# Dilated attention: the q/k tiles of two of the three dilations turned by DMA transposes and kept in token order

## The chip, the cores and the metric

The kernel runs on one core of a Trainium2 chip. The metric is device time in microseconds (us) of one execution, the median of the runs. The engines are TensorE (PE in the rows, its weight loads PEld), VectorE (DVE), ScalarE (ACT), GpSimd (POOL) and SyncE (SP), which issues most DMAs.

## The reference

A trunk of two layers over 256 tokens of width 1024, in fp32: a sparse attention layer, then a dilated attention layer, each followed by a gated feed-forward block. The change touches the dilated layer alone. It projects the normed input to q, k and v of 16 heads of 64 for each of three dilations (1, 4, 16), turns the first 16 elements of each q and k head by position, and lets each token see the tokens of its own residue class within a window. The three outputs are joined with the softmax of their log sums, which is one softmax over all three sets of scores.

```python
DIL_PATTERNS = ((128, 1), (512, 4), (2048, 16))
proj = (a @ w_in).reshape(B, S, N_DIL, 3, H, DH)
for gi, (window, dil) in enumerate(DIL_PATTERNS):
    q = partial_rope(proj[:, :, gi, 0], cos, sin)
    k = partial_rope(proj[:, :, gi, 1], cos, sin)
    v = proj[:, :, gi, 2]
    o, lse = banded_attention(to_residue(q, dil)[:, :, :, None], to_residue(k, dil),
                              to_residue(v, dil), window // dil)
    ...
alpha = jax.nn.softmax(jnp.stack(lses, axis=-1), axis=-1)
o = jnp.einsum('bshn,bshnd->bshd', alpha.astype(a.dtype), jnp.stack(outs, axis=3))
return o.reshape(B, S, H * DH) @ w_o
```

## The kernel before

Every large product is made as three matmuls of fp32r parts: each weight piece (1 MB, a slot of a ring of seven in w_raw) is split by ScalarE into a high part (w_hi, L735) and by VectorE into a low part (w_lo, L1256), two halves each. SyncE issues the loads of the pieces in order; each waits until the piece seven before it has been used. ScalarE splits a piece three ahead of the tile that TensorE works on.

The dilated layer takes its 16 heads in four groups of four. A group has tiles of 128 tokens by 512 columns, each of 24 matmuls (gemm, L1830): six q/k tiles, two for each dilation (pat 0, 1 and 2 stand for dilations 1, 4 and 16), two tiles of v for pat 0 and 1, and in groups 0 and 2 two more v tiles for pat 2. There are 36 tiles in all, numbered e. The first group takes its q/k tiles in the order pat 1, 2, 0, the others 1, 0, 2, so that in those the tiles of pat 2 come last. For v tiles the stationary operand, the turned input, is read with a step of two elements (8 bytes).

A q/k tile goes this way. ScalarE evacuates it from PSUM to stage_dil (L1103, two slots), VectorE applies the rotation in place (L1688 to L1695), TensorE turns it with four transposes in the middle of the next tile's matmuls (dil_turn, L1839), and ScalarE evacuates the turned tile (dil_turn_out, L1127 to L1136) into qk_t, in an order in which the tokens of a class lie together, with q scaled. For pat 0 the high parts go to qk_hi, and VectorE makes the low parts from PSUM and qk_hi (dil_turn_lo, L1708 and L1713).

Scores are made for 16 units, four to a group (dil_scores): a unit is two heads by 128 queries. It has eight matmuls of 64x64 in fp32 for the residue classes of pat 1 and 2 (class matmuls), whose k is read with a step of two elements, and six of 64x128x256 in fp32r for pat 0. Scores of a group are made among the tiles of the next group; those of the last group among the output projection's matmuls, the first after 18 of these with the last tile's turn in their middle. VectorE masks the scores and finds the least (L1451), ScalarE takes the exponential, VectorE divides, TensorE turns the probabilities and multiplies them with v.

GpSimd has no work in the dilated layer but two DMAs. It stores the residual h to h_rows, waits, and loads it back in another order of rows (h_permuted), which VectorE needs when it adds the output projection. In the two feed-forward blocks a hidden tile of 128x256 is turned without TensorE: GpSimd splits it into two planes of 16 bits (split_hidden, L683), ScalarE issues a DMA transpose (L1018), GpSimd merges the planes (merge_hidden, L691).

## Time and profile before

| | us |
|---|---|
| median of 3 runs | 810.12 (810.08 to 810.49) |
| profiled execution, its device time | 810.76 |
| its span, first to last instruction | 809.0 |
| dilated layer in it, tiles and attention | about 342 to 616 |

The profile is of one execution of its own. Its span leaves out some 1.8 us ahead of and behind the instructions. A duration in a timeline row runs from start to modelled end, and neighbours on TensorE overlap, so the time that one costs is read from the starts around it.

### The profile page before, as it was taken

What the parts mean: (1) busy time and instruction counts of PE and PEld (TensorE: products, weight loads), DVE (VectorE), ACT (ScalarE), POOL (GpSimd) and SP (SyncE); (2) the same over time, 40 slices, a digit from 0 to 9 for tenths busy, and PEclk for the clock granted to TensorE, in tenths of its full rate; (3) what the DMA queues carried; (4) which work ended last, traced back from release to release, by engine and by line L of the source; (5) the groups of instructions that cost most, each with busy time, mean ns of one, the idle gap of its engine ahead of it and who ended that gap; (6) DMA issues with size and microseconds to landing.
All of it is one profiled execution on the core that took longest, in us unless ns stands there. A gap on an engine that the chain in (4) does not pass through costs nothing.

```text
span 809.0 us, 11869 instructions
## 1 busy us (share of the span) xinstructions
PE 798.6 (99%) x4401; PEld 643.8 (80%) x4401; DVE 528.5 (65%) x1121; ACT 457.5 (57%) x879; POOL 102.2 (13%) x167
## 2 busy tenths in 40 slices
PE   9999999999999999999999999999999999999996
PEld 7877675788888888788888888888877888888885
DVE  6966969796565556697566665766668775655644
ACT  7836877765444444575555566555658554444431
POOL 1000005812212221000000000000000112222210
PEclk9999999999999999999999999999999999999998
DMA  9955211168886687658544535363424688678811
GB/s 318 351 184 200 86 54 53 59 189 241 242 212 191 191 238 216 188 198 269 157 157 153 160 121 192 105 208 105 157 88 172 191 248 224 173 197 236 236 21 52
DMA packets 128490, 142.24 MB, mean 176 GB/s; under 512 B 25856, under 2 KB 111920, under 8 KB 128304
## 3 DMA queue, kind: packets, MB, share of 16 engines
q1 hardware_dynamic: 107760, 132.53, 52.6%
q10 hardware_dynamic: 19680, 4.75, 3.6%
q0 software_dynamic: 992, 4.19, 1.4%
q8 instruction: 35, 0.57, 0.3%
q14 instruction: 23, 0.19, 0.1%
HBM read 134.64 MB, written 2.10 MB: 169 GB/s over the span
## 4 chain that ended last, share of the span: by engine, by line
PE 96%; DVE 2%; ACT 1%; issue 0%; POOL 0%; ACTq 0%; POOLq 0%
PE ps L1830 86%; PE ps L1839 6%; PE ps L2107 2%; PE ps L2080 2%; PE ps L2118 1%; PE ps L1892 1%; ACT junk L756 0%; DVE w_lo L1256 0%; ACT xd_hi L744 0%; ACT w_hi L735 0%; ACT probs_b L907 0%; DVE h L1580 0%; DVE h L1586 0%; DVE tmp L1584 0%; ACT p_t L922 0%
## 5 line engine op out<-in xcount | busy, mean ns | idle before, releaser
L1256 DVE TENSOR_TENSOR w_lo<-w_raw,w_hi 128x1024 fp32r<-128x1024 f32 x240 | 295.5, 1259 | 64.8 <-ACT w_hi L735 62.5
L735 ACT ACTIVATE w_hi<-w_raw 128x1024 fp32r<-128x1024 f32 x240 | 245.5, 1060 | 3.0 <-DMA w_raw<-in_ffn_w_gu 2.9
L1830 PE MATMUL ps<-w_hi,xt_hi 128*128 128x512 f32 x472 | 188.5, 401 | 0.3 <-ACT w_hi L735 0.3
L1830 PE MATMUL ps<-w_hi,xt_lo 128*128 128x512 f32 x472 | 183.5, 390 | 0.0
L1830 PE MATMUL ps<-w_lo,xt_hi 128*128 128x512 f32 x472 | 183.0, 390 | 0.0
L1830 PE MATMUL ps<-w_hi,xd_hi 128*128 128x512 f32 x288 | 117.4, 408 | 0.2 <-DVE w_lo L1256 0.2
L1830 PE MATMUL ps<-w_hi,xd_lo 128*128 128x512 f32 x288 | 113.2, 393 | 0.0
L1830 PE MATMUL ps<-w_lo,xd_hi 128*128 128x512 f32 x288 | 112.8, 392 | 0.0
L1830 PEld LDWEIGHTS ps<-w_hi,xt_hi 128*128 128x128 f32 x472 | 88.5, 188 | 25.0 <-issue 8.6
L1830 PEld LDWEIGHTS ps<-w_hi,xt_lo 128*128 128x128 f32 x472 | 88.6, 188 | 18.9
L1830 PEld LDWEIGHTS ps<-w_lo,xt_hi 128*128 128x128 f32 x472 | 88.7, 188 | 16.7 <-DVE w_lo L1256 0.3
L1002 ACT ACTIVATE silu<-ps,rs 128x256 f32<-128x256 f32 x44 | 20.9, 475 | 91.6 <-PE ps L1830 87.9
L1830 PEld LDWEIGHTS ps<-w_hi,xd_lo 128*128 128x128 f32 x288 | 54.7, 190 | 11.8
L1830 PEld LDWEIGHTS ps<-w_hi,xd_hi 128*128 128x128 f32 x288 | 54.8, 190 | 11.2 <-DVE w_lo L1256 0.4
L1830 PEld LDWEIGHTS ps<-w_lo,xd_hi 128*128 128x128 f32 x288 | 54.9, 191 | 9.8
L1830 PE MATMUL ps<-w_hi,st_hi 128*128 128x512 f32 x160 | 62.6, 391 | 0.0
L1830 PE MATMUL ps<-w_hi,st_lo 128*128 128x512 f32 x160 | 62.3, 389 | 0.0
L1830 PE MATMUL ps<-w_lo,st_hi 128*128 128x512 f32 x160 | 62.3, 389 | 0.0
L691 POOL COPY ht<-planes_t 128x512 uint16<-128x512 uint16 x36 | 33.4, 928 | 212.1 <-DMA planes_t<-planes 212.1
L1594 DVE SCALAR_TENSOR_TENSOR hs<-ps,rs,silu 128x256 f32<-128x256 f32 x44 | 21.3, 483 | 51.9 <-ACT silu L1002 51.9
L1012 ACT ACTIVATE st_hi<-ht 128x256 fp32r<-128x256 f32 x36 | 15.0, 416 | 70.8 <-PE ps L1830 42.1
L1600 DVE TENSOR_TENSOR st_lo<-ht,st_hi 128x256 fp32r<-128x256 f32 x36 | 15.2, 422 | 48.2 <-ACT st_hi L1012 48.2
(271 smaller groups left out, 984.9 us busy)
## 6 DMA issues: line engine op xcount, KB each, us to landing
w_raw<-in_ffn_w_gu SPq DMA_DIRECT2D x88, 512.0 KB, 5.6
w_raw<-in_dil_w_in SPq DMA_DIRECT2D x72, 512.0 KB, 4.6
w_raw<-in_ffn_w_down SPq DMA_DIRECT2D x44, 512.0 KB, 5.4
w_raw<-in_nsa_w_in SPq DMA_DIRECT2D x20, 512.0 KB, 7.3
w_raw<-in_nsa_w_o SPq DMA_DIRECT2D x8, 512.0 KB, 4.8
w_raw<-in_dil_w_o SPq DMA_DIRECT2D x8, 512.0 KB, 4.5
w_k<-in_nsa_cmp_wk SPq DMA_DIRECT2D x2, 1024.0 KB, 9.0
w_raw<-in_nsa_cmp_wv SPq DMA_DIRECT2D x2, 1024.0 KB, 11.5
```

The lines of the kernel that those rows point to most:

```text
L691: pool.tensor_copy(halves_of(ht[:, j % 2, m, :]), view(planes_t, (j % 2 * MT + m) * 512, [[256, 2], [1, 256]])).then_inc(ht_merged, 1)
L735: act.activation(w_hi[:, n.slot, c:c + 1024], w_raw[:, n.slot, c:c + 1024], ACT.Copy)\
L1002: act.activation(silu[:, m, :], bank(gu_bank(j, m), 0, 256), ACT.Silu, scale=rs[:, m:m + 1])\
L1012: act.activation(view(st_of(j)[0], m * P, [[S, 2], [1, P]]), ht_from(j, m), ACT.Copy)\
L1256: dve.tensor_tensor(w_lo[:, n.slot, c:c + 1024], w_raw[:, n.slot, c:c + 1024], w_hi[:, n.slot, c:c + 1024].bitcast(F32), ALU.subtract)\
L1594: dve.scalar_tensor_tensor(hs[:, m, :], bank(gu_bank(j, m), 256, 256), rs[:, m:m + 1], silu[:, m, :], ALU.mult, ALU.mult).then_inc(hs_read ...
L1600: dve.tensor_tensor(view(st_of(j)[1], m * P, [[S, 2], [1, P]]), ht_from(j, m), hi.bitcast(F32), ALU.subtract).then_inc(ht_ready, 1)
L1830: ins = pe.matmul(o, s, m, start=start, stop=stop, **kw)
L1839: ins = pe.transpose(ps[0:n, b, P * k:P * k + P], src, ident[:, 0:P])
L1892: pe.transpose(bank(3, 0, P), ident[:, 0:P], ident[:, 0:P])
L2080: pe.matmul(bank(score_bank(odd), 0, 2 * n), q_t[rows, hd // 2, m * P:(m + 1) * P], k_both[rows, :, hd // G, 0:n], start=True, stop=True). ...
L2107: pe.matmul(view(ps, OT_BANK * 512 + P * j, [[1, P]], p0=DH * odd, n=DH), v_nsa[:, i // (m + 1), i % (m + 1), hk * DH:(hk + 1) * DH], p_t2 ...
```

## The change

The 16 q/k tiles of pat 0 and 1 (BARS) are no longer turned by TensorE; the eight of pat 2 (PE_TURNS) still are. After the rotation GpSimd splits a tile of 128x512 fp32 into two planes (split_qk, 128x1024 of 16 bits), SyncE issues a DMA transpose of both planes at a fixed place among the weight loads (turn_planes, called by load), and GpSimd merges the result into qk_t, in token order (merge_qk). The planes are laid over h, so h is stored to h_rows in two parts (save_h) and loaded back when the last merge is done.

The scores read the classes of pat 1 by steps of four elements, for q and for k. For pat 0, ScalarE and VectorE make the high and low parts of a whole group's q and k once the last merge of the group is done (first_q_hi, first_lo_out, first_k_hi): q into an order in which its columns stay contiguous for the scores, k in token order, read with a step of two elements. The scale of q moves from the evacuation to the mask operation, and the constants of the mask change with it. The first scores of a group wait for the merges and for the evacuation of the pat 2 tiles, and those of pat 0 for the low parts.

```diff
@@ -117,27 +117,29 @@
 
 
 XBAR = [(1, 0), (1, 1)] + [(j, m) for j in range(2, FJ - 1) for m in range(MT)]
+DIL_BARS = 2 * MT * DIL_G
...
 def xbar_no(layer, j, m):
 
-    return len(XBAR) * layer + XBAR.index((j, m))
+    return (len(XBAR) + DIL_BARS) * layer + XBAR.index((j, m))
...
 
     tiles = [x for x in XBAR if x[1] == m]
-    return len(tiles) * layer + tiles.index((j, m)) + 1
+    return (len(tiles) + DIL_BARS // 2) * layer + tiles.index((j, m)) + 1
...
-N_TURNS = sum(x.kind == QK for x in TILES)
-
-
-def firsts_until(qk_no):
-
-    return sum(x.kind == QK and x.pat == 0 and x.qk_no <= qk_no for x in TILES)
+BARS = [x for x in TILES if x.kind == QK and x.pat < 2]
+PE_TURNS = [x for x in TILES if x.kind == QK and x.pat == 2]
+
+
+def bar_at(x):
+
+    return len(XBAR) + BARS.index(x)
...
-        h = sb("h", [P, MT, D])
+        at_h = zone(MT * D * 4)
+        h = sb("h", [P, MT, D], at=at_h)
+        planes_q = sb("planes_q", [P, 2, 1024], U16, at=at_h)
+        planes_qt = sb("planes_qt", [P, 2, 8, P], U16, at=at_h + 4096)
...
-        qk_hi = sb("qk_hi", [P, 4, 4, S], F32R, at=at_a)
+        k_parts = sb("k_parts", [P, 4, 2, 2, S], F32R, at=at_a)
...
-        qk_lo = [sb(f"qk_lo{i}", [P, S], F32R, at=at) for i, at in
-                 enumerate((at_gp + 3072, at_s + 9216, at_tmp + 3072, at_tmp + 7168))]
+        q_hi, q_lo = ([sb(f"q_{k}{hp}", [P, S], F32R, at=at) for hp, at in enumerate(homes)] for k, homes in
+                      (("hi", (at_gp + 3072, at_s + 9216)), ("lo", (at_tmp + 3072, at_tmp + 7168))))
...
+        def first_q_whole(g, hp):
+
+            return view(qk_t, (qk_slot(g, 0) * 4 + hp) * S, [[1, 2], [2, 2], [4, 64]])
+
+        def first_q_part(t, hp):
+
+            return view(t[hp], 0, [[P, 2], [64, 2], [1, 64]])
...
+            def turn_ahead_of(x):
+
+                return N_DIL + ({0: 7, 2: 10}[x.e] if x.e < 4 else 2 * x.chunk + 8 + x.m)
+
+            def turn_planes(n):
+
+                for i, x in enumerate(BARS):
+                    if turn_ahead_of(x) != n:
+                        continue
+                    if i == 0:
+
+                        sp.wait_ge(h_saved, 16 * MT)
+                        sp.wait_ge(xt_psum[2], 2 * MT)
+                        sp.wait_ge(sq_h[2], MT)
+                    sp.wait_ge(planes_ready, bar_at(x) + 1)
+                    sp.dma_start_transpose(planes_qt[:, i % 2, :, :], planes_q[:, i % 2, :])\
+                      .then_inc(planes_turned[i % 2], 16)
+
             def load(pc, *parts):
 
+                turn_planes(pc.n0)
...
+            def split_qk(x):
+
+                pool.wait_ge(roped[1], x.qk_no + 1)
+                pool.tensor_copy(view(planes_q, BARS.index(x) % 2 * 1024, [[512, 2], [1, 512]]),
+                                 halves_of(stage_dil[:, x.qk_no % 2, :])).then_inc(planes_ready, 1)
+
+            def merge_qk(x):
+
+                i, pos = BARS.index(x), qk_order(x.g).index(x.pat)
+                pool.wait_ge(planes_turned[i % 2], 16 * (xbar_of(0, FJ - 2, i % 2) + i // 2 + 1))
+
+                if x.g - (pos == 0) > 0:
+                    pool.wait_ge(scores[1], 8 * (x.g - (pos == 0)))
+                to = qk_t[:, qk_slot(x.g, x.pat), :, x.m * P:(x.m + 1) * P].bitcast(U16)
+                pool.tensor_copy(to.rearrange("p b (i k) -> p k b i", k=2),
+                                 view(planes_qt, i % 2 * 1024, [[512, 2], [P, 4], [1, P]])).then_inc(ht_merged, 1)
+
+            def save_h(m):
+
+                for half in range(2):
+                    pool.wait_ge(h_ready[2][half], m + 1)
+                pool.dma_start(h_rows[m * P:(m + 1) * P, :], h[:, m, :]).then_inc(h_saved, 16)
...
-                pool.wait_ge(h_ready[b][1], MT)
-                if b != 2:
+                    pool.wait_ge(h_ready[b][1], MT)
                     post_gain(b + 1, *nexts[b])
                 else:
 
-                    pool.wait_ge(h_ready[2][0], MT)
-                    pool.dma_start(h_rows.rearrange("(m p) c -> p m c", m=MT), h[:, :, :]).then_inc(h_saved, 16)
+                    save_h(0)
                     pool.wait_ge(h_saved, 16)
-                    pool.wait_ge(xt_psum[2], 2 * MT)
-                    pool.wait_ge(sq_h[2], MT)
+                    save_h(1)
+                    pool.wait_ge(xt_psum[2], 2)
+                    pool.wait_ge(sq_h[2], 1)
+                    for g in range(DIL_G):
+                        first, second, third, fourth = [x for x in BARS if x.g == g]
+                        split_qk(first)
+                        split_qk(second)
+                        merge_qk(first)
+                        split_qk(third)
+                        merge_qk(second)
+                        split_qk(fourth)
+                        merge_qk(third)
+                        merge_qk(fourth)
+                    pool.wait_ge(ht_merged, len(XBAR) + DIL_BARS)
...
                 if x.kind == QK:
                     if x.e in (0, 2):
                         act.wait_ge(rs_ready[2], x.m + 1)
+                    for y in BARS:
+                        if y.qk_no == x.qk_no - 2:
+                            act.wait_ge(planes_ready, bar_at(y) + 1)
                     ins = act.activation(stage_dil[:, x.qk_no % 2, :], bank(b), ACT.Copy, scale=rs[:, x.m:x.m + 1])
...
-                if x.kind != QK:
+                if x not in PE_TURNS:
                     return
-                act.wait_ge(turned[1], x.qk_no + 1)
-                at = qk_slot(x.g, x.pat) * 4 * S
-                src = (2 + x.qk_no % 2) * 512
-                qk = qk_hi if x.pat == 0 else qk_t
+                no = PE_TURNS.index(x)
+                act.wait_ge(turned[1], no + 1)
+                at = qk_slot(x.g, 2) * 4 * S
+                src = (2 + no % 2) * 512
                 for hp in range(2):
...
-                    act.activation(view(qk, at + hp * S + 32 * x.m, [[P, 2], [64, 2], [1, 32]]),
-                                   view(ps, src + P * hp, [[1, 2], [2, 2], [4, 32]]), ACT.Copy, scale=-SCALE)
+                    act.activation(view(qk_t, at + hp * S + 32 * x.m, [[P, 2], [64, 2], [1, 32]]),
+                                   view(ps, src + P * hp, [[1, 2], [2, 2], [4, 32]]), ACT.Copy)
...
+            def first_q_hi(g):
+
+                act.wait_ge(ht_merged, len(XBAR) + 4 * (g + 1))
+                for hp in range(2):
+                    ins = act.activation(first_q_part(q_hi, hp), first_q_whole(g, hp), ACT.Copy)
+                ins.then_inc(qk_hi_ready, 1)
+
+            def first_k_hi(g):
+
+                act.wait_ge(qk_lo_ready, 2 * g + 1)
+                at = qk_slot(g, 0)
+                act.activation(k_parts[:, at, 0, :, :], qk_t[:, at, 2:4, :], ACT.Copy).then_inc(qk_hi_ready, 1)
...
                 dil_evac(TILES[e - 1])
                 split(n + k, (0,))
+                if TILES[e].g > TILES[e - 1].g:
+                    first_q_hi(TILES[e - 1].g)
                 dil_attend(2 * e)
                 dil_odd_out(2 * e + 1)
                 if e == 4:
                     split(n + k, (1,))
+                if TILES[e].g > TILES[e - 1].g:
+                    first_k_hi(TILES[e - 1].g)
                 dil_turn_out(TILES[e - 1])
                 if e > 4:
...
             split(n + 3, (0,))
+            first_q_hi(DIL_G - 1)
+            first_k_hi(DIL_G - 1)
             dil_turn_out(TILES[-1])
             split(n + 3, (1,))
...
+            def mask_part(dst, w, c, n, mask, least, scale=1.0):
+
+                return dve.tensor_tensor_reduce(out=dst, in0=bank(score_bank(w), c, n), in1=mask, scale=scale,
...
-            def dil_turn_lo(x):
-
-                if x.kind != QK or x.pat:
-                    return
-                dve.wait_ge(turn_out[1], x.qk_no + 1)
-                at = qk_slot(x.g, 0) * 4 * S
-                src = (2 + x.qk_no % 2) * 512
+            def first_lo_out(g):
+
+                dve.wait_ge(qk_hi_ready, 2 * g + 1)
                 for hp in range(2):
-                    for par in range(2):
-                        to, dims = 32 * x.m + P * par, [[64, 2], [1, 32]]
-                        dve.scalar_tensor_tensor(view(qk_lo[hp], to, dims), view(ps, src + P * hp + par, [[2, 2], [4, 32]]),
-                                                 -SCALE, view(qk_hi, at + hp * S + to, dims).bitcast(F32),
-                                                 ALU.mult, ALU.subtract)
-                for hp in range(2):
-                    to, dims = x.m * 64, [[P, 2], [1, 64]]
-                    ins = dve.tensor_tensor(view(qk_lo[2 + hp], to, dims), view(ps, src + (2 + hp) * P, [[1, 2], [2, 64]]),
-                                            view(qk_hi, at + (2 + hp) * S + to, dims).bitcast(F32), ALU.subtract)
+                    ins = dve.tensor_tensor(first_q_part(q_lo, hp), first_q_whole(g, hp),
+                                            first_q_part(q_hi, hp).bitcast(F32), ALU.subtract)
                 ins.then_inc(qk_lo_ready, 1)
+                at = qk_slot(g, 0)
+                dve.wait_ge(qk_hi_ready, 2 * g + 2)
+                dve.tensor_tensor(k_parts[:, at, 1, :, :], qk_t[:, at, 2:4, :], k_parts[:, at, 0, :, :].bitcast(F32),
+                                  ALU.subtract).then_inc(qk_lo_ready, 1)
...
-                              mn[:, w % 4, 0:1])\
+                              mn[:, w % 4, 0:1], scale=-SCALE)\
...
-                if x.kind != QK:
+                if x not in PE_TURNS:
                     return
+                no = PE_TURNS.index(x)
                 pe.wait_ge(roped[1], x.qk_no + 1)
-                if x.qk_no >= 2:
-                    pe.wait_ge(turn_out[1], x.qk_no - 1)
-                    if firsts_until(x.qk_no - 2):
-                        pe.wait_ge(qk_lo_ready, firsts_until(x.qk_no - 2))
+                if no >= 2:
+                    pe.wait_ge(turn_out[1], no - 1)
                 for k in range(4):
-                    ins = turn(2 + x.qk_no % 2, k, stage_dil[:, x.qk_no % 2, P * k:P * k + P])
+                    ins = turn(2 + no % 2, k, stage_dil[:, x.qk_no % 2, P * k:P * k + P])
...
+            def head(g, pat, t, j, c, dims):
+
+                return view(qk_t, (qk_slot(g, pat) * 4 + 2 * t + j // 2) * S + c, dims, p0=DH * (j % 2), n=DH)
+
+            def class_q(g, pat, j, m, cls):
+
+                return head(g, pat, 0, j, *((m + 2 * cls, [[4, 64]]) if pat == 1 else (m * P + 64 * cls, [[1, 64]])))
+
+            def class_k(g, pat, j, m, c):
+
+                return head(g, pat, 1, j, *((m + 2 * c, [[4, 64]]) if pat == 1 else (m * P + c, [[2, 64]])))
+
+            def first_q(j, m):
+
+                rows = slice(DH * (j % 2), DH * (j % 2) + DH)
+                return [q[j // 2][rows, m * P:(m + 1) * P] for q in (q_hi, q_lo)]
+
+            def first_k(g, j):
+
+                return [view(k_parts, ((qk_slot(g, 0) * 2 + part) * 2 + j // 2) * S, [[1, 2], [2, P]],
+                             p0=DH * (j % 2), n=DH) for part in range(2)]
 
             def dil_scores(g, t):
                 (m, hp), ws = dil_unit(t), pair_units(g, t)
                 if ws[0] >= 2:
                     pe.wait_ge(masked[1], ws[0])
                 if t == 0:
-                    pe.wait_ge(qk_lo_ready, 2 * (g + 1))
+                    pe.wait_ge(ht_merged, len(XBAR) + 4 * (g + 1))
+                    pe.wait_ge(turn_out[1], 2 * (g + 1))
                 js = (2 * hp, 2 * hp + 1)
                 for pat in (1, 2):
                     for cls in range(2):
-                        for odd, w in enumerate(ws):
-                            j, c = 2 * hp + odd, cls if pat == 1 else 1 - cls
+                        for j, w in zip(js, ws):
+                            c = cls if pat == 1 else 1 - cls
                             mm(ps[64 * cls:64 * cls + 64, score_bank(w), 256 + c:DIL_N:2],
-                                     head(g, pat, 0, j, m * P + 64 * cls, 64), head(g, pat, 1, j, m * P + c, 64, 2),
-                               True, True)
+                               class_q(g, pat, j, m, cls), class_k(g, pat, j, m, c), True, True)
+                if t == 0:
+                    pe.wait_ge(qk_lo_ready, 2 * (g + 1))
                 for j, w in zip(js, ws):
-                    mm(bank(score_bank(w), 0, S), first_hi(g, 0, j, m * P, P), first_hi(g, 1, j, 0, S), True, False)
+                    mm(bank(score_bank(w), 0, S), first_q(j, m)[0], first_k(g, j)[0], True, False)
                 for j, w in zip(js, ws):
-                    mm(bank(score_bank(w), 0, S), first_hi(g, 0, j, m * P, P), first_lo(1, j, 0, S), False, False)
+                    mm(bank(score_bank(w), 0, S), first_q(j, m)[0], first_k(g, j)[1], False, False)
                 for j, w in zip(js, ws):
-                    mm(bank(score_bank(w), 0, S), first_lo(0, j, m * P, P), first_hi(g, 1, j, 0, S), False, True)\
+                    mm(bank(score_bank(w), 0, S), first_q(j, m)[1], first_k(g, j)[0], False, True)\
```

## Rows read from the trace of the kernel before

**Rows 1.** The page: busy us (share of the span) and instructions of each engine.
```profile
PE 798.6 (99%) x4401; PEld 643.8 (80%) x4401; DVE 528.5 (65%) x1121; ACT 457.5 (57%) x879; POOL 102.2 (13%) x167
```

**Rows 2.** The page: the chain that ended last, shares by engine.
```profile
PE 96%; DVE 2%; ACT 1%; issue 0%; POOL 0%; ACTq 0%; POOLq 0%
```

**Rows 3.** Windows: a stretch of the dilated layer; busy us per engine, clock, DMA share, GB/s.
```profile
416.00:462.00 46.00, 46.00 (x324) 37.61 (x324) 29.16 (x74) 26.64 (x55) 0.00 (x0) 1.00 0.46 146
```

**Rows 4.** Groups by line and form, TensorE: busy us, mean ns.
```profile
L1839 PE MATMUL ps<-ident,stage_dil 128*128 128x128 f32 x96 | 14.7, 275 | 0.0
```

**Rows 5.** Timeline of TensorE around one block: start us, us, engine, operation.
```profile
433.58 0.39 PE L1830 MATMUL ps<-w_hi,xd_lo 128*128 128x512 f32 x1
433.81 0.60 PE L1839 MATMUL ps<-ident,stage_dil 128*128 128x128 f32 x4
434.16 0.48 PE L1830 MATMUL ps<-w_hi,xd_hi 128*128 128x512 f32 x1
434.48 0.40 PE L1830 MATMUL ps<-w_lo,xd_hi 128*128 128x512 f32 x1
```

**Rows 6.** Timeline, 586 to 591 us: the end of the last group's tiles and the first scores.
```profile
586.04 1.05 ACT L735 ACTIVATE w_hi<-w_raw 128x1024 fp32r<-128x1024 f32 x1
...
587.19 1.23 DVE L1256 TENSOR_TENSOR w_lo<-w_raw,w_hi 128x1024 fp32r<-128x1024 f32 x1
...
587.93 0.45 ACT L1127 ACTIVATE qk_t<-ps 128x128 f32<-128x128 f32 x2 [0.84 <-PE ps L1839]
...
588.26 0.40 ACT L1136 ACTIVATE qk_t<-ps 128x256 f32<-128x256 f32 x1
...
589.91 0.46 PE L1830 MATMUL ps<-qk_t 64*64 64x64 f32 x16
...
590.30 0.39 PE L1830 MATMUL ps<-qk_hi 64*128 64x256 f32 x2
...
590.85 0.50 PE L1830 MATMUL ps<-w_hi,ot_hi_s 128*128 128x512 f32 x1
```

**Rows 7.** Timeline of TensorE in a v tile: two matmuls, 20 starts apart.
```profile
385.24 0.40 PE L1830 MATMUL ps<-w_hi,xd_hi 128*128 128x512 f32 x1
...
389.95 0.40 PE L1830 MATMUL ps<-w_hi,xd_lo 128*128 128x512 f32 x1
```

**Rows 8.** Tiles planes and planes_t: durations ns min/median/max, first and last start.
```profile
L683 POOL COPY planes<-hs x36: 605/742/1677, 172.8 to 778.3; 128x512 uint16<-128x512 uint16 x36
...
L1018 ACTq DMA_TRANSPOSE planes_t<-planes x36: 1205/1207/1293, 174.3 to 779.1; - x36
L691 POOL COPY ht<-planes_t x36: 757/768/1828, 183.5 to 781.6; 128x512 uint16<-128x512 uint16 x36
...
DMA to landing us min/median/max: 2.4/6.1/9.1
```

**Rows 9.** Timeline, around 573 us: the last weight issue and the rotation's last step.
```profile
572.18 0.92 SPq L502 DMA_DIRECT2D w_raw<-in_ffn_w_gu  x2
...
573.28 0.29 DVE L1695 TENSOR_TENSOR stage_dil<-rope_a,rope_b 128x128 f32<-128x128 f32 x1
```

**Rows 10.** A weight load of SyncE, ScalarE's split of that piece, and landings of w_raw.
```profile
357.70 0.92 SPq L502 DMA_DIRECT2D w_raw<-in_dil_w_in  x2
...
367.95 2.02 ACT L735 ACTIVATE w_hi<-w_raw 128x1024 fp32r<-128x1024 f32 x2
...
DMA to landing us min/median/max: 3.5/4.7/7.6
```

**Rows 11.** Timeline: nearest rows for copies and subtractions of 512 and 256 columns.
```profile
584.29 0.62 ACT L1146 ACTIVATE ot_hi_s<-ps 128x512 fp32r<-128x512 f32 x1
...
585.59 0.68 DVE L1731 TENSOR_TENSOR ot_lo_s<-ps,ot_hi_s 128x512 fp32r<-128x512 f32 x1
...
605.75 0.42 DVE L1731 TENSOR_TENSOR xt_lo<-ps,xt_hi 128x256 fp32r<-128x256 f32 x1 [0.20 <-ACT xt_hi L1146]
```

**Rows 12.** Timeline of VectorE: the first use of the residual after the dilated layer.
```profile
610.36 0.69 DVE L1565 TENSOR_TENSOR tmp<-ps,g_post 128x512 f32<-128x512 f32 x1
```

More of the change, by code:

```diff
@@ L654, in _ @@
                     p0 = mask_dil[rows, m, 0:256].rearrange("p (b q) -> p b q", b=2)
[L656 removed]
+                    link(pool.affine_select(out=p0, in_=p0, compare_op=ALU.is_ge, fill=NEG / SCALE,
                                             base=m + 2 * cls, pattern=[[-1, 2], [-2, P]], channel_multiplier=4))
[L658 removed]
+                    link(pool.affine_select(out=p0, in_=p0, compare_op=ALU.is_ge, fill=NEG / SCALE,
                                             base=128 - m - 2 * cls, pattern=[[1, 2], [2, P]], channel_multiplier=-4))
@@ L661, in _ @@
                 p2 = mask_dil[rows, 0, 257 - cls:DIL_N:2]
-                link(pool.affine_select(out=p1, in_=p1, compare_op=ALU.is_ge, fill=-NEG,
+                link(pool.affine_select(out=p1, in_=p1, compare_op=ALU.is_ge, fill=NEG / SCALE,
                                         base=0, pattern=[[-1, 64]], channel_multiplier=1))
-                link(pool.memset(p2, -NEG))
+                link(pool.memset(p2, NEG / SCALE))
                 for d in range(0, 64, 4):
@@ L1447, in cmp_probs @@
                    .then_inc(pc_ready, 1)
-            def mask_part(dst, w, c, n, mask, least):
-                return dve.tensor_tensor_reduce(out=dst, in0=bank(score_bank(w), c, n), in1=mask, scale=1.0,
+            def mask_part(dst, w, c, n, mask, least, scale=1.0):
+                return dve.tensor_tensor_reduce(out=dst, in0=bank(score_bank(w), c, n), in1=mask, scale=scale,
                                                 scalar=INF, op0=ALU.add, op1=ALU.min, accum_out=least)
```

24 lines of the change are left out of this document (6 added, 18 removed).

## The prediction

> **What bounds the kernel now.** I read the page's busy times, the chain that ended last, a window of the dilated stage, and then the timeline there. TensorE is busy for 99% of the span, while VectorE, ScalarE and GpSimd stand at 65, 57 and 13% [rows 1]. The chain agrees: 96% of it is matmuls, almost none of it waits [rows 2]. So the time is the sum of what TensorE is given, and the other engines matter only where TensorE comes to wait for them. The stretch from 416 to 462 us shows the same inside the dilated layer: TensorE 46.00 of 46.00 us at full granted clock, VectorE 29 us, ScalarE 27 us, GpSimd nothing [rows 3].
>
> **What is removed from TensorE.** 96 transposes of stage_dil run before, four for each of 24 q/k tiles [rows 4]; the 8 tiles of pat 2 keep theirs, so 16 blocks of four go. A block is cheaper than its four durations of 0.27 us. The neighbouring matmuls start 0.23 us apart (433.58 to 433.81); the block starts at 433.81, the next matmul at 434.16 and the one after at 434.48, not at 433.81 and 434.04 as they would without it [rows 5]. The difference is 434.48 - 434.04 = 0.44 us. 16 x 0.44 = 7.0 us. Their waits cost nothing before, so there is nothing more to gain. If only the 0.35 us between the block's start and the next matmul came back, the gain would be 5.6 us; that is its lower end.
>
> **What the scores' new strides cost.** A unit of scores (16 of them, four to a group) takes 0.94 us: from 589.91 to 590.30 its eight class matmuls, to 590.85 its six of pat 0, and the first weight matmul follows [rows 6]. Counts and shapes stay. Two steps change: q and k of pat 1 are read 16 bytes apart (before: q contiguous, k 8 bytes), which touches half of the 0.39 us; k of pat 0, the moving operand of all six, is read 8 bytes apart, before contiguous. If a step halved the rate of what it touches, the first would cost 0.39/2 x 16 = 3.1 us and the second 0.55 x 16 = 8.8 us. The lower end of both is nothing. The nearest rows are mild: before, the class k already go in at 8 bytes within those 0.39 us, and the matmuls of a v tile, whose stationary operand is read at 8 bytes, start (389.95 - 385.24)/20 = 0.236 us apart [rows 7] against 0.23 at contiguous ones, so 3% at most. The class matmuls are 16 records within 0.39 us, 24 ns for each, and four tiles of 64x64 lie side by side in the array: their number seems to pace them rather than their reads. I take nothing for both, being nearest to these rows, and keep 3.1 and 8.8 us for the range.
>
> The Trainium skill bears on this (SBUF — State Buffer, "Door 1: The DMA port swizzle", its note on cachelines): a line of SBUF is 16 bytes, and full rate needs at least two hits on a line. By it, 8 bytes in fp32 are free and 16 bytes are not, so the first price is due in part or whole and the second isn't. No row here has TensorE reading at 16 bytes. By the rule in full the sum below would be 3.1 us higher.
>
> **The new way of a tile.** ScalarE's evacuation and VectorE's rotation stay. Then GpSimd splits the tile into two planes, SyncE issues a DMA transpose, GpSimd merges. The kernel has the same three steps at half the size in the feed-forward layers [rows 8]: the split takes 0.74 us in the median (0.61 to 1.68), the issue 1.21, issue to landing 6.1 (2.4 to 9.1), the merge 0.77 (to 1.83). Twice the size: split 1.5, merge 1.5, issue 2.4, landing 4.8 at best (2 x 2.4), 12.2 if the median doubled, 18.2 if the longest did. GpSimd gets 16 x 3.0 = 48 us in a stage of some 230 us (354 to 588) in which it does nothing.
>
> The critical tile is the last one of pat 0 of a group. In the last group its rotation ends at 573.57; the issue of weights ahead of it was at 572.18 and took 0.92 us, so SyncE's queue is free [rows 9]. Split to 575.1. The values are wanted by ScalarE at 587.09, after its weight split that starts at 586.04 [rows 6]; one removed block lies between, so 0.4 us sooner. For issue to landing that leaves 587.1 - 0.4 - 575.1 - 1.5 = 10.1 us, less 0.3 for three semaphores: about 9.8. I expect some 5 to 7, since the weights of 572.18 should be down by then and none follow till the transpose is out. So the transfer is hidden. The cover is 9.8 us in the last group and close to that in the others, which have the same order of tiles; the first group has four v tiles more.
>
> **SyncE's queue.** The waits for planes sit between weight loads. The load behind a tile's second transpose waits for a piece that is used half a tile later still, so it isn't held. One load is: the first transpose waits for the squares of h, and ahead of the load that starts at 357.70 it puts up to 2.4 us. ScalarE splits that piece at 367.95 [rows 10], 10.2 us after the issue. The median landing of a piece there is 4.7 us and the longest 7.6, so 2.4 us more still fit, nearly always. Nothing is charged. Every other load behind a transpose is issued over three tiles before its split, each of 24 matmuls or 5.5 us.
>
> **ScalarE and VectorE.** 16 evacuations after the turn go (each about 0.73 us, from 587.93 to 588.66 [rows 6]), and 8 rounds of the low parts; per group come two 128x256 and one 128x512 on each of the two. Both lose work in total. But the new operations stand in a row at the end of a group: q high (ScalarE), q low (VectorE), k high (ScalarE), and only then the evacuation of the last turned tile, which the scores now wait for. For the last group: q high from 587.09, 2 x 0.40, to 587.9; VectorE is in its weight split to 588.42, then q low 2 x 0.42, to 589.26; k high 0.62 [rows 11], to 589.9; the evacuation 0.73, to 590.6. TensorE wants it at 589.91, so it stands for 0.7 us, or about 0.5 since operations in a row start some 0.1 us before the one ahead ends. I take 0.6, with 0.2 and 1.2 as ends. k low, 0.68 from 589.9, is ready at 590.6 and wanted 0.39 us after the scores start: no wait. In the other groups a whole tile of 24 matmuls (5.5 us) and a block of transposes lie between that last evacuation and the scores, here only 18 matmuls (4.1 us) and a block. The 1.4 us more cover the 0.6: no charge there. Behind TensorE in that wait stand the output projection and all later turns of probabilities; they just follow by 0.6.
>
> **Home of h.** The planes live in h, so its reload waits for the last merge, about 584; VectorE wants it at 610.36 [rows 12]. That is 26 us for 1 MB, of which a load of half that size took 4.7 us in the median.
>
> **Sum.** -7.0 + 0.6 = -6.4 us. The profiled execution took 810.76 us (span 809.0, 1.8 us around it), the median of the runs is 810.12, 0.6 below. A change of 6.4 us takes the profiled span to 802.6 and the median to 803.7. A measurement of this kernel tells 0.2%, 1.6 us, from no change.
>
> **Rivals.**
> *The class scores pay for the 16-byte step.* It costs at most 3.1 us: 806.9, still faster. For it: no row shows that step as free. Against: those matmuls seem bound by their number. Here stands the cacheline rule cited above. 0.11.
>
> *The k stream of pat 0 pays for the 8-byte step.* Up to 8.8 us: 812.5 at worst; with half of it, 808.1. To undo the gain it needs 6.4/16 = 0.40 us more per unit, 73% of the 0.55. Against it stands the 0.236 us of the strided v tiles. 0.08, half of it within 0.2% or slower.
>
> *The transposes land late* (the rival on the slower side). The place is ScalarE's wait for the merges before q high. Beyond 9.8 us from issue to landing every us holds ScalarE, and TensorE soon after, in up to three groups. It eats the gain where 3 x (L - 9.8) = 6.4, at L = 11.9 us; at the doubled median of 12.2 the time is 803.7 + 7.2 = 810.9, at the doubled longest 803.7 + 25 = 829. For it: landings of 7 to 9 us occur at half the size. Against: those go beside weight loads, and at the critical place SyncE has none under way. 0.13, two thirds of it with L over 11.4.
>
> *The forecast*, all of the saving but for a short wait: 0.66, own range 802.6 to 805.5. 0.02 is left for what I don't see.
>
> **How the numbers follow.** The range begins at 802.5 (0.45 a block and a wait of 0.2, less some slack) and reaches 808.5: the forecast (0.66), the class scores (0.11) and the mild halves of the other two (0.08) are 0.85 in it. Faster by over 0.2%: 0.66 + 0.11 + 0.04 + 0.02 = 0.83. Within 0.2% (808.5 to 811.7): 0.07. Slower: 0.10.
>
> **What would show it.** Transposes of stage_dil at 32, and around removed places matmuls 0.23 us apart. A unit of scores still 0.94 us; 1.1 would be the class step, 1.5 the k stream. TensorE idle for 0.6 us once, before the first scores of the last group, put down to ScalarE. Issue to landing of the transposes under 9.8 us and no wait of q high for GpSimd's merge. SyncE's issue of a transpose about 2.4 us. What would make me wrong is TensorE waiting at the start of three groups, or weight splits on ScalarE that wait for a landing.

## The result, and the profile after

The changed kernel takes 816.22 us (median of four runs: 814.17, 816.16, 816.29, 816.54) against 810.31 us before on the same chip: ratio 1.0066, interval 1.0048 to 1.0084. It is slower by 0.66%, where the forecast was 803.7 us and faster. The profiled execution is the one of 816.54 us, span 814.8 against 809.0, so 5.8 us have to be found.

The page after, busy times and the chain by engine:

```profile
PE 801.9 (98%) x4337; PEld 642.1 (79%) x4337; DVE 543.6 (67%) x1085; ACT 453.2 (56%) x843; POOL 146.9 (18%) x200
PE 94%; DVE 3%; ACT 2%; issue 1%; POOL 0%; ACTq 0%; POOLq 0%; DVEq 0%
```

TensorE has 64 instructions fewer than in [rows 1], yet it is busy for 3.3 us more: what remains must have become dearer. The waits of TensorE from 355 to 625 us, with their sum in us, their number and the longest (there were none in this stretch before):

```profile
PE ps L1910 <- ACT qk_t L1204: 1.2, 1, 1.2
PE ps L1919 <- DVE probs_dil L1569: 1.2, 4, 0.3
```

The transposes of stage_dil in that trace are the 32 that were foreseen:

```profile
L1919 PE MATMUL ps<-ident,stage_dil x32: 270/272/328, 360.5 to 588.9; 128*128 128x128 f32 x32
```

**The removed blocks.** As a mark serves the first weight matmul behind the wait for w_lo at the start of the dilated layer. Before and after:

```profile
348.73 0.50 PE L1830 MATMUL ps<-w_hi,xd_hi 128*128 128x512 f32 x1 [0.20 <-DVE w_lo L1256]
```
```profile
349.35 0.50 PE L1910 MATMUL ps<-w_hi,xd_hi 128*128 128x512 f32 x1 [0.15 <-DVE w_lo L1341]
```

From there to the first scores it was 407.70 - 348.73 = 58.97 us; it is 406.54 - 349.35 = 57.19. Four of the sixteen blocks lay in this stretch, 1.78/4 = 0.445 us each.

**The unit of scores.** The first unit in the timeline of TensorE, before and then after:

```profile
407.70 0.46 PE L1830 MATMUL ps<-qk_t 64*64 64x64 f32 x16
408.10 0.39 PE L1830 MATMUL ps<-qk_hi 64*128 64x256 f32 x2
408.32 0.28 PE L1830 MATMUL ps<-qk_lo,qk_hi 64*128 64x256 f32 x2
408.44 0.28 PE L1830 MATMUL ps<-qk_hi,qk_lo 64*128 64x256 f32 x2
408.64 0.51 PE L1830 MATMUL ps<-w_hi,xd_hi 128*128 128x512 f32 x1
```
```profile
406.54 0.62 PE L1910 MATMUL ps<-qk_t 64*64 64x64 f32 x16
407.09 0.71 PE L1910 MATMUL ps<-k_parts,q_hi 64*128 64x256 f32 x4
407.62 0.41 PE L1910 MATMUL ps<-k_parts,q_lo 64*128 64x256 f32 x2
407.96 0.51 PE L1910 MATMUL ps<-w_hi,xd_hi 128*128 128x512 f32 x1
```

From the first class matmul to the next weight matmul it took 0.94 us, now 1.42. The class part grew from 0.40 to 0.55 us (406.54 to 407.09), the pat 0 part from 0.54 to 0.87. The other units show the same (one, at the lower clock of below, takes 1.57): 16 x 0.48 = 7.7 us, more than the blocks gave.

**The last group.** The rows of ScalarE, VectorE and TensorE that answer to [rows 6]:

```profile
587.32 1.05 ACT L800 ACTIVATE w_hi<-w_raw 128x1024 fp32r<-128x1024 f32 x1
...
588.26 1.23 ACT L1212 ACTIVATE q_hi<-qk_t 128x256 fp32r<-128x256 f32 x2
...
588.82 1.23 DVE L1341 TENSOR_TENSOR w_lo<-w_raw,w_hi 128x1024 fp32r<-128x1024 f32 x1 [0.47 <-ACT w_hi L800]
...
589.97 1.12 DVE L1787 TENSOR_TENSOR q_lo<-qk_t,q_hi 128x256 fp32r<-128x256 f32 x2
...
591.12 0.63 ACT L1219 ACTIVATE k_parts<-qk_t 128x512 fp32r<-128x512 f32 x1 [1.62 <-DVE q_lo L1787]
591.66 0.42 ACT L1195 ACTIVATE qk_t<-ps 128x128 f32<-128x128 f32 x2
...
591.97 0.39 ACT L1204 ACTIVATE qk_t<-ps 128x256 f32<-128x256 f32 x1
...
592.50 0.39 PE L1910 MATMUL ps<-qk_t 64*64 64x64 f32 x4 [1.24 <-ACT qk_t L1204]
```

The chain is the predicted one, and twice as long: the scores could have started at about 591.2, 0.33 us behind the weight matmul of 590.86, and start at 592.50. Then comes something that the prediction had not priced. Windows of TensorE behind that wait (behind the window stand its length, TensorE's busy us with the instructions, the granted clock as a share of the full one, the DMA share and GB/s):

```profile
592.00:594.00 2.00, 1.50 (x23) 1.00 0.09 31
594.00:596.00 2.00, 2.00 (x7) 0.69 0.00 0
596.00:598.00 2.00, 2.00 (x20) 0.50 0.00 0
598.00:600.00 2.00, 2.00 (x17) 0.96 0.00 0
```

For some 3 us, from the middle of the second window to just behind the third, TensorE was granted its lower level, 1.2 GHz in place of 2.4 (0.50).

**GpSimd beside VectorE.** Around 424 us, in this order: the rotation's last step, GpSimd's split into planes, VectorE's normalization of probabilities, TensorE's turn of them, and the next normalization:

```profile
423.80 0.29 DVE L1780 TENSOR_TENSOR stage_dil<-rope_a,rope_b 128x128 f32<-128x128 f32 x1
...
424.16 1.04 POOL L736 COPY planes_q<-stage_dil 128x1024 uint16<-128x1024 uint16 x1 [35.21 <-DVE stage_dil L1780]
...
424.33 1.08 DVE L1569 TENSOR_SCALAR probs_dil<-probs_dil,rl 128x384 f32<-128x384 f32 x1
...
425.46 0.55 PE L1919 MATMUL ps<-ident,probs_dil 128*128 128x128 f32 x3 [0.30 <-DVE probs_dil L1569]
...
426.65 0.42 DVE L1569 TENSOR_SCALAR probs_dil<-probs_dil,rl 128x384 f32<-128x384 f32 x1
```

The same normalization takes 1.08 us while GpSimd copies and 0.42 when it doesn't, and TensorE waits for it four times (425.46, 448.65, 552.97, 576.15). The copy itself takes 1.04 us, as the median of the 16 does.

**The transposes** of planes_q (durations in ns, then issue to landing in us):

```profile
L524 SPq DMA_TRANSPOSE planes_qt<-planes_q x16: 1237/1238/2047, 357.0 to 575.9; - x16
...
DMA to landing us min/median/max: 3.2/5.2/6.5
```

### The profile page after: what moved, and what is told of

Read it like the earlier page. It is cut to its first block, busy times and chain, and to the rows that moved or that the text cites. A ratio compares the mean times of both kernels' runs of the same rounds, so it can differ in the third digit from the quotient of the medians.

```text
span 814.8 us, 11730 instructions
## 1 busy us (share of the span) xinstructions
PE 801.9 (98%) x4337; PEld 642.1 (79%) x4337; DVE 543.6 (67%) x1085; ACT 453.2 (56%) x843; POOL 146.9 (18%) x200
## 4 chain that ended last, share of the span: by engine, by line
PE 94%; DVE 3%; ACT 2%; issue 1%; POOL 0%; ACTq 0%; POOLq 0%; DVEq 0%
PE ps L1910 85%; PE ps L1919 5%; PE ps L2187 2%; PE ps L2160 2%; PE ps L1972 1%; PE ps L2198 1%; DVE probs_dil L1569 1%; DVE w_lo L1341 0%; ACT stage_dil L1171 0%; ACT junk L821 0%; ACT xd_hi L809 0%; ACT w_hi L800 0%; DVE h L1665 0%; DVE h L1671 0%; DVE tmp L1669 0%
## 5 line engine op out<-in xcount | busy, mean ns | idle before, releaser
L1341 DVE TENSOR_TENSOR w_lo<-w_raw,w_hi 128x1024 fp32r<-128x1024 f32 x240 | 308.8, 1310 | 51.4 <-ACT w_hi L800 49.4
L723 POOL COPY ht<-planes_t 128x512 uint16<-128x512 uint16 x36 | 28.8, 801 | 178.2 <-DMA planes_t<-planes 178.2
L715 POOL COPY planes<-hs 128x512 uint16<-128x512 uint16 x36 | 32.2, 896 | 102.4 <-DVE hs L1679 102.4
L736 POOL COPY planes_q<-stage_dil 128x1024 uint16<-128x1024 uint16 x16 | 19.8, 1238 | 170.3 <-DVE stage_dil L1780 170.3
```

The lines of the kernel that those rows point to most:

```text
L715: pool.tensor_copy(view(planes, (j % 2 * MT + m) * 512, [[256, 2], [1, 256]]), halves_of(hs[:, m, :]))\
L723: pool.tensor_copy(halves_of(ht[:, j % 2, m, :]), view(planes_t, (j % 2 * MT + m) * 512, [[256, 2], [1, 256]])).then_inc(ht_merged, 1)
L736: pool.tensor_copy(view(planes_q, BARS.index(x) % 2 * 1024, [[512, 2], [1, 512]]), halves_of(stage_dil[:, x.qk_no % 2, :])).then_inc(plane ...
L1341: dve.tensor_tensor(w_lo[:, n.slot, c:c + 1024], w_raw[:, n.slot, c:c + 1024], w_hi[:, n.slot, c:c + 1024].bitcast(F32), ALU.subtract)\
```

## The experiments

The mark above is at 349.35 us in the changed kernel's trace and between 348.2 and 349.0 in the others, so stretches are counted from it. "Unit us" is what a unit of scores takes. "Last group" is the start of its first scores, "16th" that of the last unit. Each ratio is to the kernel before on the same chip as that run. The four runs that take the reads apart were executed once each and are told in the text.

| run | median us | ratio to before (interval) | unit us | last group | 16th |
|---|---|---|---|---|---|
| before | 810.3 to 811.0 | 1 | 0.94 | 241.18 | 254.73 |
| changed kernel | 816.22 | 1.0066 (1.0048 to 1.0084) | 1.42 | 243.15 | 259.42 |
| a_old_reads | 807.18 | 0.9957 (0.9942 to 0.9972) | 0.94 | 237.46 | 251.00 |
| b_new_steps | 818.13 | 1.0093 (1.0076 to 1.0110) | 1.42 | 246.98 | 261.91 |
| a_tail | 813.25 | 1.0034 (1.0020 to 1.0047) | 1.42 | 241.84 | 256.78 |
| a_short_copies | 812.44 | 1.0021 (1.0012 to 1.0031) | 1.42 | 241.17 | 256.11 |
| a_held | 812.88 | 1.0024 (1.0014 to 1.0034) | 1.42 | 241.13 | 256.08 |
| a_tail_held | 811.34 | 1.0007 (0.9998 to 1.0017) | 1.42 | 239.83 | 254.77 |
| v_order | 806.69 | 0.9946 (0.9930 to 0.9963) | 0.94 | 237.10 | 250.65 |
| v_all | 803.48 | 0.9908 (0.9893 to 0.9923) | 0.94 | 234.09 | 247.62 |

### The strides in the changed kernel and in the one before

```diff
-                view(k_parts, ..., [[1, 2], [2, P]], ...)            # k of pat 0
+                view(k_parts, ..., [[1, S]], ...)
-                (m + 2 * cls, [[4, 64]]) if pat == 1 else ...        # q of pat 1
+                m * P + 64 * cls, [[1, 64]]
-                (m + 2 * c, [[4, 64]]) if pat == 1 else ...          # k of pat 1
+                m * P + c, [[2, 64]]
```

(Shortened here, the comments are mine. This is a_old_reads, in the changed kernel; b_new_steps makes the reverse edits in the kernel before. Neither moves the data, so both mix up tokens.)

> The changed kernel with one edit: TensorE reads the scores' operands at the steps of the kernel before (q of pat 1 contiguous, its k at two elements, k of pat 0 contiguous). Same counts, shapes and waits; the scores mix up tokens, so the output is not the reference's. Theory, the strides cost the 0.48 us that a unit of scores grew by: unit back to 0.94 us, 16 x 0.48 = 7.7 us less, 808.5 us. Rival, GpSimd's copies or the DMA transposes slow TensorE's reads: the unit stays near 1.42 us and the time near 816.2.

> The kernel before with one edit: the scores' operands are read at the steps of the changed kernel (q and k of pat 1 at four elements, k of pat 0 at two). All data stay where they are, so the scores mix up tokens and the output is not the reference's. Strides theory: unit of scores 0.94 to 1.42 us, 810.3 + 7.7 = 818.0 us. Rival (contention with work that only the changed kernel has): unit 0.94, time 810.3.

The unit falls to 0.94 us in the one and rises to 1.42 in the other, where the dilated layer has neither planes nor GpSimd copies. The kernel before with the new steps, the first unit:

```profile
407.67 0.62 PE L1830 MATMUL ps<-qk_t 64*64 64x64 f32 x16
408.22 0.48 PE L1830 MATMUL ps<-qk_hi 64*128 64x256 f32 x2
408.52 0.41 PE L1830 MATMUL ps<-qk_lo,qk_hi 64*128 64x256 f32 x2
408.75 0.42 PE L1830 MATMUL ps<-qk_hi,qk_lo 64*128 64x256 f32 x2
409.09 0.50 PE L1830 MATMUL ps<-w_hi,xd_hi 128*128 128x512 f32 x1
```

The stretch to the 16th unit holds 15 units: 261.91 - 254.73 = 7.18 us, 0.479 each. The strides are the whole of it; contention with GpSimd or the transposes has no part. a_old_reads came out 9.0 us faster than the changed kernel where 7.7 were expected: 259.42 - 251.00 = 8.42 us to the 16th unit, 7.2 from 15 units and some 1.3 because the clock didn't fall in this execution (below), though the wait ahead of it stayed (1.26 us). The rest of the 9.0 is the 16th unit (0.5) and scatter between executions.

### Which operand pays

```diff
-    [[1, 2], [2, P]]   # k of pat 0
+    [[1, S]]           # a_k0_contig
+    [[1, 4], [4, 64]]  # a_k0_step4
```

a_c1_q and a_c1_k make the second and the third edit of the diff before this one alone. These four runs are single executions; their readings rest on the timeline rows, in which the sixteen units of a run agree within 0.03 us, and not on their times.

> The changed kernel, but k of pat 0, the moving operand of six matmuls in a unit of scores, is read contiguous instead of 8 bytes apart (scores mix up tokens). Theory, this step costs 0.31 of the 0.48 us: a unit from one row of class matmuls to the next weight matmul 1.42 - 0.31 = 1.11 us, the pat 0 durations back from 0.41 to 0.28 us, the run 5.0 us shorter. Rival, the step is free and the layout of q (hi and lo) or k_parts costs it: unit 1.42 us.

> The changed kernel, but q of pat 1, the stationary operand of the class matmuls, is read contiguous instead of 16 bytes apart (tokens mixed up). Theory A, the moving side pays as it does for pat 0: class matmuls stay at 0.55 us, unit 1.42. Theory B, the stationary side pays: 0.39 us and unit 1.26.

> The changed kernel, but k of pat 1, the moving operand of the class matmuls, is read 8 bytes apart as before instead of 16 (tokens mixed up). Theory A, the moving side pays: class matmuls 0.39 us, unit 1.26, 16 x 0.16 = 2.6 us less. Theory B, the stationary side pays: 0.55 and 1.42.

> The changed kernel, but k of pat 0 is read by steps of four elements (16 bytes) instead of two (tokens mixed up). It asks for the rate of a moving operand at 16 bytes. Theory, any step in the moving operand halves its rate: unit 1.42 us as with 8 bytes. Rival, the rate goes with the step: q low by k from 0.41 to some 0.7 us, unit 2.0 us or more.

a_k0_contig (809.06 us, one run): the pat 0 part is back,

```profile
405.40 0.62 PE L1910 MATMUL ps<-qk_t 64*64 64x64 f32 x16
405.95 0.50 PE L1910 MATMUL ps<-k_parts,q_hi 64*128 64x256 f32 x4
406.29 0.28 PE L1910 MATMUL ps<-k_parts,q_lo 64*128 64x256 f32 x2
406.50 0.51 PE L1910 MATMUL ps<-w_hi,xd_hi 128*128 128x512 f32 x1
```

and the unit takes 1.10 us: the 8-byte step of k costs 0.32. The layouts of q and of k_parts are the changed kernel's here, and the pat 0 part is 0.55 us as before, so they cost nothing. (The run came out 7.2 us shorter where 5.0 were expected; its clock didn't fall either.) a_k0_step4 (816.36 us) has the same 0.41 us for the same matmuls and a unit of 1.42: at 16 bytes the moving operand is as slow as at 8 and no slower.

```profile
407.13 0.41 PE L1910 MATMUL ps<-k_parts,q_lo 64*128 64x256 f32 x2
407.47 0.50 PE L1910 MATMUL ps<-w_hi,xd_hi 128*128 128x512 f32 x1
```

For the class matmuls both theories missed. With q contiguous (a_c1_q, 814.80 us) they take 0.49 us in place of 0.55, with k at 8 bytes (a_c1_k, 814.31 us) 0.52, with both 0.39. Neither side carries the 0.16 us by itself, and each edit alone saves less than its share. Why the two don't add was not followed further. With q contiguous a k at 8 bytes, as before, costs nothing there: in v_order (below), where k of pat 1 is contiguous too, the class part takes the same 0.39 us.

### The order at the end of the last group

```diff
             dil_evac(TILES[-1])
-            split(n + 3, (0,))
             first_q_hi(DIL_G - 1)
-            first_k_hi(DIL_G - 1)
             dil_turn_out(TILES[-1])
+            first_k_hi(DIL_G - 1)
+            split(n + 3, (0,))
             split(n + 3, (1,))
...
             dil_rope(TILES[-1])
-            split(n + 3, (0,))
             first_lo_out(DIL_G - 1)
+            split(n + 3, (0,))
```

> The changed kernel with another order at the end of the last group: ScalarE makes q high, evacuates the last turned tile and makes k high ahead of its weight split, VectorE makes q low ahead of its own. Theory: the 1.4 us in which TensorE stood before the first scores of the last group go, and with them the half clock at about 594.5 to 598 (about 2 us): 816.2 - 3.4 = 812.8 us, granted clock 1.00 from 588 to 617. Rival, the clock fell for another reason: only the wait goes, 814.8 us. Rival, the weight splits put off take its place: a wait of TensorE for w_hi or w_lo at about 592 to 597, no gain.

Measured 813.25 us, 3.0 less. The wait is gone (243.15 to 241.84, 1.31 us) and so is the lower clock (last group to 16th unit: 16.27 to 14.94, 1.33 us). The weight splits that were put off are not waited for.

### GpSimd's copies

```diff
-    view(planes_q, ..., [[512, 2], [1, 512]]), halves_of(stage_dil[:, x.qk_no % 2, :])
+    n = 512 if BARS.index(x) < 2 else 16
+    view(planes_q, ..., [[512, 2], [1, n]]), halves_of(stage_dil[:, x.qk_no % 2, 0:n])
```

(a_short_copies, shortened here: 14 of the 16 splits, and in the same way 8 of the 16 merges, are cut to 1/32, so data are left out.) a_held keeps every copy whole; GpSimd only waits for VectorE's next normalization first:

```diff
                 pool.wait_ge(roped[1], x.qk_no + 1)
+                for g, t in pairs_at(2 * x.e + 2, 1):
+                    pool.wait_ge(normed[1], pair_units(g, t)[0] + 1)
```

> The changed kernel with 14 of 16 splits into planes and 8 of 16 merges on GpSimd cut to 1/32 of their columns; issue order, transposes and waits stay. Data are left out, so the output is not the reference's. Theory, GpSimd's copies hold VectorE's operations and so the probabilities: VectorE's normalizations at 424 and 447 us back from 1.08 to 0.42 us, the four waits of TensorE for probabilities (0.3 us each) gone, about 1.2 us less: 815.0 us. Rival, those waits are VectorE's own new order (low parts made in a row): they stay, 816.2 us. If copies also slow TensorE's reads, the unit of scores of the last groups falls below 1.42 us.

> The changed kernel with one edit: GpSimd begins the split of a tile only after VectorE's next normalization of probabilities, where one follows the rotation. All work stays. Theory, the split running beside that normalization holds it and TensorE: normalizations back to 0.42 us, the four waits gone, 4 x 0.5 = 2.0 us less, 814.2 us (the wait of 1.2 us in the last group stays; whether the clock falls after it is open, which moves the run by 1.3 us more). Rival, the later transposes are not hidden any more: a wait of ScalarE's q high for GpSimd's merge, time 816 or more.

> The changed kernel with the end order and the hold together, strides left as they are. Theory: 816.2 - 2.6 - 2.0 = 811.6 us, TensorE waits nowhere in the dilated layer, and what is left over the kernel before is units 16 x 0.48 less blocks 16 x 0.44 = +0.6 us. Rival, the two overlap: 812.9 as with the hold alone.

VectorE's normalizations from 400 to 625 us, in the changed kernel and with the copies cut (busy us, mean ns); the kernel before has 13.5 and 421 too:

```profile
L1569 DVE TENSOR_SCALAR probs_dil<-probs_dil,rl 128x384 f32<-128x384 f32 x32 | 17.9, 560 | 1.1
```
```profile
L1571 DVE TENSOR_SCALAR probs_dil<-probs_dil,rl 128x384 f32<-128x384 f32 x32 | 13.5, 421 | 1.1
```

All four waits go in both runs. In a_held the copy has moved behind one normalization, onto the weight split and the next normalization:

```profile
423.44 0.42 DVE L1571 TENSOR_SCALAR probs_dil<-probs_dil,rl 128x384 f32<-128x384 f32 x1
423.78 1.22 DVE L1343 TENSOR_TENSOR w_lo<-w_raw,w_hi 128x1024 fp32r<-128x1024 f32 x1
423.99 1.90 POOL L738 COPY planes_q<-stage_dil 128x1024 uint16<-128x1024 uint16 x1 [37.01 <-DVE probs_dil L1571]
424.12 0.49 PE L1921 MATMUL ps<-ident,probs_dil 128*128 128x128 f32 x3
...
425.11 1.00 DVE L1571 TENSOR_SCALAR probs_dil<-probs_dil,rl 128x384 f32<-128x384 f32 x1
```

So my expectation that the normalizations return to 0.42 us was wrong: six of 32 still take 1.0 to 1.3 us, but none that TensorE is about to read. The rows also show which of the two pays. The split of 424.16 above, started ahead of the normalization, took its 1.04 us, and the normalization was stretched; here the copy starts behind VectorE's weight split, takes 1.90 us, and the weight split keeps its 1.22. In the changed kernel a weight split that starts at 438.81, 0.06 us behind a copy, takes 2.05. a_tail to a_tail_held is 241.84 to 239.83, 2.01 us for four waits: 0.50 each, though the rows show 0.30 of idle time. In a_short_copies and a_held the wait of 1.24 us before the last group is still there, and the clock stays at 1.00 behind it in their traces. That fits their gains (3.8 and 3.3 us, where 1.2 and 2.0 were expected): 2.0 for the waits and 1.3 for the clock make 3.3; the 0.5 more of a_short_copies stays open.

### The costs taken out without leaving data out

```diff
-    to = qk_t[:, qk_slot(x.g, x.pat), :, x.m * P:(x.m + 1) * P].bitcast(U16)
-    pool.tensor_copy(to.rearrange("p b (i k) -> p k b i", k=2), view(planes_qt, ..., [[512, 2], [P, 4], [1, P]]))
+    to = qk_t[:, slot, :, :].bitcast(U16).rearrange("p b (r i k) -> p k b r i", k=2, r=4)
+    half = qk_t[:, slot, :, :].bitcast(U16).rearrange("p b (r i k) -> p k b r i", k=2, r=2)
+    def put(b, bs, r, n, to):
+        return pool.tensor_copy(to[:, :, b:b + bs, :, x.m * n:(x.m + 1) * n],
+                                view(planes_qt, at + b * P, [[512, 2], [P, bs], [1, r], [r, n]]))
+    put(0, 4, 4, 32, to)            # pat 1: q and k by class
+    put(0, 2, 4, 32, to)            # pat 0: q by class
+    put(2, 2, 2, 64, half)          # pat 0: k by parity
```

(Shortened here: slot stands for qk_slot(x.g, x.pat), at for i % 2 * 1024. With it, TensorE reads q and k of pat 1 and k of pat 0 contiguous, and q high and q low read runs of 64 elements. This alone is v_order; v_all adds the order of a_tail and the hold of a_held.)

> The changed kernel with the first of these edits alone: merges write the order in which TensorE then reads contiguous columns. Theory: unit 0.94 us, 7.7 us less, 808.5 us; q high and q low now read runs of 64 elements, 0.4 us each again in place of 0.6, so the wait of the last group falls from 1.2 to about 0.4 to 0.8 us and the half clock behind it may go: down to 806.5 us.

> The changed kernel with three edits that keep every result: GpSimd's merges write pat 1 by residue class, q of pat 0 by class and k of pat 0 by parity, so that TensorE reads contiguous columns (the same number of elements, 20 merges' instructions in place of 16); the order at the end of the last group of the run called a_tail; the hold of the splits of the run called a_held. Theory, the three costs are separate and add: 816.2 - 7.7 (unit 0.94 us) - 2.6 (wait and half clock) - 2.0 (waits for probabilities) = 803.9 us, which is about 0.9% under the kernel before. Rival, a merge with 64-byte runs is much slower on GpSimd, holds VectorE longer or makes q high wait: unit 0.94, but new waits of TensorE, 806 or more.

v_order measures 806.69 us: units of 0.94, and a last wait of 0.91 us in place of 1.24, since VectorE's q low takes 0.42 us for 128x256 at runs of 64 elements and took 0.60 at 16-byte steps (ScalarE's q high 0.41 for 0.66). v_all measures 803.48 us where the sum said 803.9. TensorE waits for nothing from 355 to 625 us, and the page reads

```profile
PE 791.0 (99%) x4337; PEld 636.6 (79%) x4337; DVE 543.5 (68%) x1085; ACT 451.3 (56%) x843; POOL 156.4 (20%) x208
```

The merges are 24 instructions (8 + 16), not the 20 that the expectation says; GpSimd is busy for 156.4 - 146.9 = 9.5 us more than in the changed kernel, and nothing of it reaches TensorE. Of these, the new order of the merges is 3.9 (30.7 to 34.6; in v_order, without the hold, 35.3), the held splits 3.5 (19.8 to 23.3); the rest lies outside the dilated layer, where the kernels are alike. To the 16th unit the stretch is 254.73 - 247.62 = 7.11 us shorter than before: the sixteen blocks, 7.0 us, and nothing else.

## Why the prediction was wrong

**The step that failed** is "What the scores' new strides cost", in "I take nothing for both, being nearest to these rows". The two cost 7.7 us: 0.32 x 16 = 5.1 for k of pat 0 (bounds 0 to 8.8), 0.16 x 16 = 2.6 for the classes (bounds 0 to 3.1). Both lay within the bounds, and both were named as rivals, but each as an alternative to the other. Had they been added, the upper end would have been 11.9 us above the forecast. So the sign that the prediction gave (1.5 us for a unit would be the k stream) would have misled too: the 1.42 us are both costs, each in part. The row that misled is the strided v tile of 0.236 us [rows 7]: there the *stationary* operand is strided, and in pat 0 it is the *moving* one. The other nearest row, the class k at 8 bytes, is a moving operand, but in a group of small matmuls that with q contiguous take 0.39 us at either step. No row before had a long moving operand that was strided, and a mild price from rows that differ in just that was no price at all.

The cacheline note of the Trainium skill (SBUF — State Buffer, "Door 1: The DMA port swizzle") wants two hits on a line of 16 bytes; read so, as the prediction does, 8 bytes are free in fp32 and 16 are not. The same note also gives "4 fp32" as how far a stride is free, by which neither would cost. These runs agree with neither reading for a moving operand: 0.41 us at 8 bytes, 0.41 at 16, 0.28 contiguous.

**The blocks**: right, 0.445 us each against 0.44. **SyncE's queue, the transposes, the home of h**: right; issue to landing 3.2 to 6.5 us with 9.8 allowed, no wait of ScalarE for a merge. The issue was taken at 2.4 us and took 1.24 in the median.

**The wait of the last group**: the right place and chain, the term mis-sized, 1.31 us for 0.6. Counted from ScalarE's weight split, VectorE's own split started about 0.3 us later than the sum has it (why, the rows don't show), and q low took 1.12 us for the 0.84 put down. q high took 1.23 for 0.80, which had room. These two were priced from contiguous rows [rows 11] though they read at 16-byte steps.

**GpSimd's copies**: I booked 48 us on an idle engine and charged nothing. They are 50.5 us from 350 to 590 us, beside a VectorE that works too, and four of them lie on a normalization that TensorE reads next: 2.0 us. No rival covered it; the prediction looked at queues and forgot that two engines can slow each other. The trace before had the sign of it: the merge of 0.77 us in the median took up to 1.83 [rows 8], and that longest one, at 245.08, starts within two weight splits of VectorE (243.93 to 246.29).

**The clock**: 1.3 us more in the profiled execution, priced nowhere in the prediction.

**Small slips**, which change nothing: 803.7 + 3.1 is 806.8 and not 806.9, and the chance of "faster by over 0.2%" counts one of the two mild shares of 0.04 that the chance of the range counts both.

The sum over the profiled executions, from the mark to the 16th unit: sixteen blocks -7.0, fifteen units +7.2, four waits +2.0, the last wait +1.3, the clock +1.3, in all +4.8 us; measured 259.42 - 254.73 = +4.7. The 16th unit adds 0.5, and 0.6 arose ahead of the mark (348.73 to 349.35). That is the 5.8 us. The 0.6 are scatter and not the change's: kernels that are alike up to the mark have it anywhere from 348.2 to 349.4.

**Open** is when the clock falls. The kernel alone doesn't seem to decide it: the changed kernel's four executions took 816.54, 814.17, 816.16 and 816.29 us at mean granted clocks of 0.995, 0.997, 0.995 and 0.996, so it probably didn't fall in the second (only the first has a trace). A wait of about 1.25 us stands at the same place in eight traces; 1.2 GHz follows in the changed kernel, in a_k0_step4 and in a_c1_q, and not in a_old_reads, a_k0_contig, a_held, a_short_copies or a_c1_k. Two windows of the same length behind it, in a_c1_q and in a_c1_k (columns as above):

```profile
592.00:596.00 4.00, 4.00 (x15) 0.57 0.00 1
```
```profile
593.00:597.00 4.00, 4.00 (x34) 1.00 0.00 0
```

Without the wait (a_tail, a_tail_held, v_all) it was not seen at this place.

## What to carry to other kernels

When a change moves the cost of an order from one engine to the way in which TensorE reads, price the moving operand by a row in which a moving operand of that length has that step; where there is none, keep the full bound in the sum, and add the bounds of all such terms. Put the reordering where there is slack: GpSimd's merges, writing runs of 32 or 64 elements, took 3.9 to 4.6 us more in all, and TensorE then kept the whole gain. An idle engine isn't free for its neighbour: place a long GpSimd copy behind the VectorE operation that TensorE waits for next.

## What the runs showed of the hardware

- A moving operand of 64x256 at a step of 8 or of 16 bytes took 0.41 us, contiguous 0.28. The class part of a unit (eight of 64x64, of which the four of pat 1 were changed) took 0.39 us with q contiguous and k at 8 bytes, 0.49 with q contiguous and k at 16, 0.52 with q at 16 and k at 8, 0.55 with both at 16.
- Where a GpSimd copy of 128x1024 of 16 bits (1.04 us) and a VectorE operation overlapped, the one that started second was stretched in the rows above: a normalization of 128x384 to 1.08 us from 0.42 and a weight split to 2.05 from 1.22 behind a copy, a copy to 1.90 behind a weight split.
- VectorE's subtraction of 128x256 took 0.60 us with its source at 16-byte steps and 0.42 at runs of 64 elements; ScalarE's copy of it 0.66 and 0.41.
- A stall of TensorE for probabilities cost 0.50 us where the row shows 0.30 of idle time.
- A DMA transpose of 128x1024 of 16 bits was issued in 1.24 us in the median, nearly as one of 128x512 (1.21) in [rows 8].
